# A two-layer hybrid transformer block: values computed for two heads at a time, and part of the conditioning product moved from TensorE to VectorE

## The reference

```python
zx = hx @ w_in[layer]
oa = softmax_attend(q, ka_all, va_all, MLA_SCALE)      # "mla": 4 heads, values 64 wide, latent and context keys
ob = window_gqa_sink(bq, bk, bv, bkc, bvc, sink)       # "swa": 4 query heads on 2 key/value heads, window, sink
oc = diff_attend(dq, dk_all, dv_all, lam)              # "diff": 4 heads, difference of two softmaxes
x = x + mx[2] * rms_norm(concat(oa, ob, oc, od) @ w_out[layer], ...)   # od: pooling group
x = x + mx[5] * rms_norm(hier_moe(modulate(...)), ...)  # 16 experts, top 2 of 4 in the chosen group
```

## Time and profile before

| | |
|---|---|
| Time of three runs | 1197.9, 1199.62, 1202.74 us; median 1199.62 |
| Profiled execution: time, span | 1200.96 us, 1199.1 us |
| Mean granted TensorE clock, share of full | 0.903 |
| TensorE matmul, busy | 950.8 us (79%) |
| VectorE busy | 316.3 us (26%) |
| ScalarE busy | 266.5 us (22%) |
| GpSimd busy | 171.0 us (14%) |
| Moved by DMA | 323.04 MB, mean 269 GB/s |

### The profile page before, as it was taken

How to read it: one execution, slowest core, us unless ns; L and a number is a source line. 1 busy time by engine, 2 the same in 40 slices (tenths; PEclk the granted TensorE clock), 3 DMA queues, 4 the chain that set the end, 5 groups by cost and what they waited for, 6 DMA issues and landing times. The chain is left out here.

```text
span 1199.1 us, 23394 instructions
## 1 busy us (share of the span) xinstructions
PE 950.8 (79%) x8976; PEld 601.0 (50%) x8977; DVE 316.3 (26%) x893; ACT 266.5 (22%) x712; POOL 171.0 (14%) x256
## 2 busy tenths in 40 slices
PE   4899998999997699989974289998996585655561
PEld 2454646766554466656752166657754353422240
DVE  1100064457434211111110420046635110000003
ACT  4121033546332111101100241024632100000001
POOL 0010025000021222211210220013001211100011
PEclk9999997999997799999997599998997788877796
DMA  9982333570175799999999945230129999999983
GB/s 376 333 254 101 140 141 141 211 247 1 34 283 208 274 372 410 410 411 410 411 411 404 357 160 234 107 140 1 38 89 371 374 410 409 410 410 410 409 326 136
DMA packets 97333, 323.04 MB, mean 269 GB/s; under 512 B 11946, under 2 KB 22964, under 8 KB 90996
## 3 DMA queue, kind: packets, MB, share of 16 engines
q1 hardware_dynamic: 70528, 279.19, 59.0%
q0 software_dynamic: 9600, 31.81, 7.8%
q10 hardware_dynamic: 17140, 11.13, 3.0%
HBM read 309.58 MB, written 18.81 MB: 274 GB/s over the span
## 5 line engine op out<-in xcount | busy, mean ns | idle before, releaser
L825 PE MATMUL psum<-weights,lat 128*32 128x256 f32 x2688 | 181.3, 426 | 96.7 <-DMA weights<-in_exp_w_gu_dram 59.5
L825 PEld LDWEIGHTS psum<-weights,lat 128*32 128x32 f32 x2688 | 108.8, 121 | 163.9 <-issue 131.5
L508 PE MATMUL psum<-hT,weights 128*128 128x512 f32 (+1 forms) x336 | 120.7, 518 | 5.6 <-ACT lat L1000 3.2
L1607 DVE STREAM_TRANSPOSE lat<-lat 128x256 f32<-128x256 f32 x66 | 29.4, 446 | 355.1 <-PE psum L825 342.6
L1169 ACT ACTIVATE lat<-psum 128x128 f32<-128x128 f32 x64 | 17.7, 277 | 357.6 <-PE psum L825 355.4
L508 PEld LDWEIGHTS psum<-hT,weights 128*128 128x128 f32 x336 | 64.0, 192 | 59.3 <-issue 49.1
L838 PE MATMUL psum<-weights,lat 128*32 128x256 f32 x1344 | 83.7, 387 | 4.7 <-issue 4.0
L659 PE MATMUL psum<-weights,R 128*128 128x64 f32 x480 | 68.8, 286 | 11.3 <-ACT R L1084 7.1
L1851 POOL DMA_INDIRECT lat<-h_rows,slot_col x68 | 66.5, 978 | 53.9 <-POOL slot_col L1848 53.0
L1380 DVE TENSOR_REDUCE st<-psum 128x1 f32<-128x512 f32 (+1 forms) x96 | 56.7, 599 | 61.9 <-PE psum L628 28.3
L659 PEld LDWEIGHTS psum<-weights,R 128*128 128x128 f32 x480 | 64.2, 205 | 16.1 <-ACT R L1084 10.9
(11 more groups left out here) (260 smaller groups left out, 1161.0 us busy)
## 6 DMA issues: line engine op xcount, KB each, us to landing
weights<-in_exp_w_gu_dram SPq DMA_DIRECT2D x44, 2048.0 KB, 23.9
weights<-in_ada_w_dram SPq DMA_DIRECT2D x24, 2048.0 KB, 8.7
weights<-in_exp_w_down_dram SPq DMA_DIRECT2D x22, 2048.0 KB
hT<-in_exp_w_gu_dram SPq DMA_DIRECT2D x10, 2048.0 KB
R<-in_exp_w_gu_dram SPq DMA_DIRECT2D x10, 2048.0 KB, 25.7
spare_w<-in_exp_w_down_dram SPq DMA_DIRECT2D x10, 2048.0 KB, 24.3
weights<-in_w_in_dram SPq DMA_DIRECT2D x6, 2048.0 KB, 16.5
weights<-in_w_out_dram SPq DMA_DIRECT2D x4, 2048.0 KB, 9.1
```

What stands on the lines that cost most here:

```text
L508: mm = nc.tensor.matmul(t[:, lo:hi], w[:, k, col:col + P], hT[:, k, lo:hi], start=(k == 0), stop=(k == KD - 1))
L825: mm = nc.tensor.matmul(gu_ps[BLK * j:BLK * j + BLK, 0:256], xgT[:, k, :], w[:, k % 4, j, :, :, :], start=(k == 0), stop=(k == KD - 1), sk ...
L1607: nc.vector.transpose(xgT[:, :, :].rearrange("p k s -> p (k s)"), xg[par]).then_inc(x_ready, 1)
```

## The change

**Values by pairs.** For mla and swa units the probabilities are scaled by the reciprocal of their sum before they are turned (VectorE, in `weigh`, in place). The values product then has V as stationary operand, 64 columns wide, and the turned probabilities as the moving one. Two heads are computed together, one in each column half of the array, so that the bank holds the output already turned, head by head in partition halves; ScalarE copies it straight into `mixT` (`pair_out`). `om`, `merge` and VectorE's output scaling stay for diff units alone. There are four `probT` buffers instead of two for mla and swa.

**Layer 1's items 4 to 11.** `ada_fold` on VectorE multiplies each k-block (128 x 2048) with the column of `silu_c` for the latent stream and adds it up in `ada_acc`; `ada_sum` on TensorE then sums over the partitions with a matrix of ones. Group 1 is folded once VectorE has scaled the last rows and the first stream is turned, and is summed after `bq0`; group 2 is folded after the latent is normalised, and is summed after `dv0`. Item 6 waits for the residual, where item 7 did, and four buffers change. As items now stay in `W[0]` until VectorE has used them, ScalarE waits for item 4 before it copies the keys, for item 7 before the diff queries and for item 10 before the latent queries, and GpSimd waits for item 4 before it clears `bqz`.

```diff
-                  (("ada", 1, 6), 1), (("ada", 1, 7), 0), (("in", 1, 3), 3), (("ada", 1, 8), 0), (("ada", 1, 9), 4),
-                  (("ada", 1, 10), 0), (("ada", 1, 11), 5), (("out", 1, 0), 3), (("out", 1, 1), 4)]
+                  (("ada", 1, 6), 0), (("ada", 1, 7), 2), (("in", 1, 3), 3), (("ada", 1, 8), 0), (("ada", 1, 9), 4),
+                  (("ada", 1, 10), 0), (("ada", 1, 11), 4), (("out", 1, 0), 3), (("out", 1, 1), 5)]
...
+            def ada_sum(S, L, r):
+                pe.wait_ge(*at("folded", L, r))
+                reuse(B_ADA, ("ada_sb", L, r))
+                for g in range(4):
+                    mm = nc.tensor.matmul(psum[32 * g:32 * g + 32, B_ADA, :], ones[:, 0:32], ada_acc[:, g * 512:(g + 1) * 512],
+                                          start=True, stop=True, skip_group_check=True)
+                mm.then_inc(*mark(S, ("ada_sum", L, r)))
...
-                        for i in (5, 6):
-                            ada_item(S + "_ada", ("ada", 1, i))
...
-                        ada_item(S + "_ada", ("ada", 1, 7))
...
-                        if used and L:
-                            for i in {1: (8,), 2: (9, 10), 3: (11,)}[c]:
-                                ada_item(S + "_ada", ("ada", 1, i))
-                            if c == 1:
-                                ada_turn(S + "_turn", 1, 1)
+                        if L and name == "bq0":
+                            ada_sum(S + "_ada", 1, 1)
+                        if L and name == "dk1":
+                            ada_turn(S + "_turn", 1, 1)
+                        if L and name == "dv0":
+                            ada_sum(S + "_ada", 1, 2)
...
+                def pair_values(u):
+                    kind, qt, h = U[u]
+                    n, k0 = (4, 0) if qt < 2 else (2, 2)
+                    pe.wait_ge(*at("probT", L, u - 1))
+                    pe.wait_ge(*at("probT", L, u))
+                    if qt == 0 and h == 1:
+                        pe.wait_ge(*at("v", L, kind))
+                    t = take("o", L, u, banks=spare(ring))
+                    for i in range(n):
+                        for b in range(2):
+                            v = {"mla": vas[L][:, k0 + i, (h - 1 + b) * 64:(h + b) * 64],
+                                 "swa": bvs[L][:, k0 + i, (h // 2) * 64:(h // 2) * 64 + 64]}[kind]
+                            mm = nc.tensor.matmul(t[64 * b:64 * b + 64, 0:P], v, turned(L, u - 1 + b)[:, i, :],
+                                                  start=(i == 0), stop=(i == n - 1), skip_group_check=True)
+                    mm.then_inc(*mark(S, ("filled", "o", L, u - 1), ("filled", "o", L, u)))
...
                 if L:
-                    ada_item("pe_comb", ("ada", 1, 4))
                     pe.wait_ge(*at("banks_out", L - 1))
                     turn_combined("pe_comb", L, 0)
...
+                def pair_out(u):
+                    kind, qt, h = U[u]
+                    copy(S, mixT[:, 2 * KINDS.index(kind) + h // 2, qt * P:(qt + 1) * P], ("o", L, u), P)
...
+            def ada_fold(S, L, r):
+                for k in range(KD):
+                    it = ("ada", L, 4 * r + k // 2)
+                    w, c = staged(it)[:, k % 2, :, :].rearrange("p g n -> p (g n)"), silu_c[:, k, 0:1]
+                    used = [("used", item_no[it])] if k % 2 else []
+                    if k % 2 == 0:
+                        v.wait_ge(*at("staged", item_no[it]))
+                    if k == 0:
+                        ts(ada_acc, w, c, None, ALU.mult).then_inc(*mark(S, ("fold", L, r, k)))
+                    else:
+                        v.wait_ge(*at("fold", L, r, k - 1))
+                        stt(ada_acc, w, c, ada_acc, ALU.mult, ALU.add)\
+                            .then_inc(*mark(S, ("fold", L, r, k), *used, *([("folded", L, r)] if k == KD - 1 else [])))
...
                 if L:
+                    ada_rows(S, 1, 1)
+                    ada_fold(S, 1, 2)
+                    ada_columns(S, 1, 1)
                     ada_rows(S, 1, 2)
...
+                    if kind != "diff":
+                        v.wait_ge(*at("rinv", L, u))
+                        p = prob[u % (AHEAD + 1)][:, 0:nk]
+                        ts(p, p, s_[:, 7:8], None, ALU.mult).then_inc(*mark(S, ("prob", L, u)))
...
                 if L:
-                    ada_rows("v_seam", 1, 1)
-                    ada_columns("v_seam", 1, 1)
+                    v.wait_ge(*at("filled", "yT", 1, 0, KD // 2 - 1))
+                    ada_fold("v_seam", 1, 1)
```

More of the change, by code:

```diff
@@ L230, in hybrid_block @@
         prob2 = part(R1, 3 * NTOK, NTOK)
-        probT = [part(R1, (4 + i) * NTOK, NTOK, "p (k q) -> p k q", k=4) for i in range(2)]
         rope_c = [part(R1, 6 * NTOK + i * SEQ, SEQ) for i in range(2)]
         rope_s = [part(R1, 7 * NTOK + i * SEQ, SEQ) for i in range(2)]
+        ada_acc = part(R1, 0, 2 * D)
         h_scaled = [part(R1, i * D, D) for i in range(2)]
@@ L253, in hybrid_block @@
         om = [part(lat, i * 4 * 256, 4 * 256, "p (q c) -> p q c", q=4) for i in range(2)]
+        probT = [part(r, o + i * NTOK, NTOK, "p (k q) -> p k q", k=4) for r, o in ((R1, 4 * NTOK), (lat, 2 * NTOK)) for i in range(2)]
         PADW = 288
@@ L354, in uses, with turned, turned_before @@
             return len(range(place, N_EXP, 3))
+        def turned(L, u):
+            return probT[u % (2 if units(L)[u][0] == "diff" else 4)]
+        def turned_before(L, u):
+            first = 2 * (len(units(L)) // 3)
+            if u < first:
+                return u - 4
+            return first - 4 + (u - first) if u < first + 2 else u - 2
         def units(L):
@@ L656, in values @@
                     for i in range(n):
[L657 to L659 removed]
+                        mm = nc.tensor.matmul(t[:, 0:64], turned(L, u)[:, i, :], dvs[L][:, k0 + i, h * 64:h * 64 + 64], start=(i == 0), stop=(i == n - 1))
                     mm.then_inc(*mark(S, ("filled", "o", L, u)))
[L662 to L670 removed]
                 per = len(U) // 3
```

62 lines of the change are left out of this document (30 added, 32 removed).

## The result

The changed kernel takes 1180.35 us (median of four runs, 1178.45 to 1636.07; the highest one was disturbed, with a granted clock of 0.554, and is not in the ratio, and the median of the other three is 1178.66) against 1198.76 us for the kernel before on the same chip: a ratio of 0.9837, 95% interval [0.9801, 0.9872]. A second submission, `after_again`, gave 1177.94 us and 0.9851 [0.9808, 0.9895]. The forecast of 1176 us with 1168 to 1190 around it holds. The profiled execution took 1178.45 us, its span is 1176.6, 22.5 less than before; 24.2 were forecast.

What follows compares the result with a forecast made beforehand. TensorE bounds the seam and attention, with VectorE loaded at attention's starts; weight traffic bounds the experts. Savings of 13.0 (seam), 7.0 (layer 0) and 4.2 (layer 1), 24.2 us, off 1200.96, less 1.3 to the median, give 1176 us, range 1168 to 1190.

Steps and rivals of the forecast that it cites:

- Part 1, the seam: Between the layers: taking layer 1's items 4 to 11 off TensorE saves 13.0 us.
- Items 5 and 6 lie where TensorE would otherwise wait for that chain: nothing for them: In the seam: removing these two items saves nothing, since TensorE would wait there for the chain behind the first turning.
- The folds: VectorE in the seam: 2.4 us a step, ends near 717.5 and 762, hidden, some 1.5 us to spare at the second.
- Rivals B and E: Seam: second fold or its loads late, 1182 us, chance 0.1; first fold late or blocking ScalarE, 1188 us, 0.03.
- Part 2, the price of a pair: Values product in attention: 16 instructions at 0.058 us plus 0.1, so 1.03 us a pair, 0.68 saved.
- Rival A: Values product: column halves no faster, 0.110 us an instruction as in bq, a full pair 1.86 us; 1189 us, chance 0.15.
- Part 3, the step that failed: Attention: VectorE's scaling of probabilities, about 0.45 us a unit, is hidden in steady windowed units but not at stage starts.
- Rival C: Attention: VectorE's scaling binds at the contended 0.72 us, and both starts lose 2 us more each; 1181 us, chance 0.1.
- The starts: Start of each attention stage: longer VectorE queue from the new scaling costs 1.2 us in layer 1, 0.7 in layer 0.
- Layer 0: Its attention saves 7.0 us: full units 4.1, context-only 1.1, half-clock pairs 0.7, merges' transposes 1.75, less 0.7 at the start.
- Rival D: Attention: emptier TensorE stays longer at half clock; 1206 us if 30 us of full-rate work run so; chance 0.04.
- One listed sign of being wrong: Granted clock of 0.5 past the attention stages' starts would show the forecast wrong.

Runs made afterwards that it cites:

- `a_pairs_only`: Changed kernel with the folds undone: items 4 to 11 on TensorE again, in the old order of loads; values by pairs stay. 1188.95 us.
- `b_fold_only`: Changed kernel with the pairs undone: `om` and `merge` back, probabilities unscaled; the folds on VectorE stay. 1181.31 us.
- `e_halves_apart`: Changed kernel with all of one head's values instructions before the other's, instead of alternating; median 7.5 us above the changed kernel's second submission.
- `c_pairs_later`: Changed kernel with TensorE multiplying a pair one step later and ScalarE taking its output one step later; 1166.91 us.
- `d_copy_first`: Changed kernel with ScalarE copying the turned probabilities before the next exponential, for non-differential units; 1166.51 us.
- `h_split_on_act`: `d_copy_first` with the quarter scalings of the late differential queries moved from VectorE to ScalarE; 1154.94 us.
- `k_all`: `h_split_on_act` plus seven additional matmuls, result unused, ahead of the second turning in the seam; 1156.21 us.
- `m_before_split`: Kernel before the change, with only the late differential queries' quarter scalings moved from VectorE to ScalarE; 1186.31 us against 1199.57.

## Why the prediction held, and where it did not

**The total** is right, partly by luck. The forecast took 13.0 us from the seam, 7.0 from layer 0 and 4.2 from layer 1. The spans show 10.4, 13.8 and 0.1; the rest, 2.2 lost behind layer 1's attention and 0.4 gained elsewhere, makes 22.5. Two terms fell short, and the clock of layer 0's attention made up for them.

**Part 1, the seam: right in mechanism, 2.6 us too large.** Item 4 ahead of the first turning was worth 5.9 us (from layer 0's third pair of loads to the turning, 265.3 before and 259.4 after) against 5.4. The items in the busy stretch less the sums (1.0 us each against 0.9) were worth 6.9 between ckv's end and layer 1's first scores, where 9.1 - 1.8 + 0.3 = 7.6 stood. Most of what was missing is between the two: the second turning and ckv ran wholly or in part at the half clock, 1.7 us more for ckv and 0.7 in the chain ahead of it. "Items 5 and 6 lie where TensorE would otherwise wait for that chain: nothing for them" counted their time and gave the clock after them no term; with them there, ckv had taken 3.69 us in the kernel before, but 6.66 in `a_pairs_only`. So these 2.4 us are the clock's, and whether the items' going caused them is not shown. Between `a_pairs_only` and `after_again` the seam is 12.6 us shorter, between the kernel before and `b_fold_only` 9.5; the forecast's 13.0 is at the upper end.

**The folds**: step (2.4), both ends, the hiding and the sums without a wait came as written. VectorE did wait for weights, 3.77 us in the first fold and 1.21 to 1.40 three times in the second, inside the margin. Rivals B and E are refuted by the missing brackets at L495 and by the seam's gain of 10.4 us.

**Part 2, the price of a pair: right** (1.03 us against 1.03), and `e_halves_apart` shows that having both halves in flight is what brings it. The exact match is luck: 16 x 0.054 is 0.86 us and going in and out 0.17, where 0.93 and 0.1 stood. Rival A is refuted. Its bound, bq's 0.110 us, is indeed bq's moving columns.

**Part 3, the step that failed**: "Probabilities are turned three units after their scores, so the longer path is hidden." The distance was counted in units, where it had to be counted in the orders of two engines. Before, every step had a values product of 0.84 us, and the copy of unit i - 4 was needed one step after it was turned. Now even steps have no product, odd steps need the copies of two units, and the younger of them stands in ScalarE behind an exponential that itself waits for maxima. This cost 0.72 us a pair in steady windowed units, all of the 0.68 that a pair saved, and more before the pairs at the stages' starts. `c_pairs_later` and `d_copy_first` give it back, 11 us. A period is then 4.05 us where 3.94 was forecast. Some 0.09 of that stand in the turning ahead of a pair, which in `c_pairs_later` takes 0.53 us (802.75 to 803.28) against 0.44 for the other one (805.38 to 805.82): going into the split array costs something ahead of the pair as well, and no term had it. Rival C named the right place for the wrong cause: a doubled scaling costs steady units nothing. Its price of 1181 us is near the measured 1180.35 by chance.

**The starts**: the forecast put the loss to the new scaling, 1.2 us in layer 1 and 0.7 in layer 0. In layer 1 TensorE's idle time ahead of the pairs among the windowed scores rose from 3.4 to 6.6 us, so by 3.2; in `d_copy_first` it is 4.4, so 1.0 more than before. The term was nearly right for what VectorE's queue adds, and the other 2.2 us are the copy's place again. The stalls themselves were there before the change (3.92 us in layer 0 and 2.21 in layer 1). Layer 1's whole account: 6.2 us of work gone, and 3.2 us of idle time more at the start, 1.7 before pairs among the windowed scores and 1.2 behind them.

**Layer 0**: against `b_fold_only` the pairs gained 7.3 us (1.5 of it the clock at most), where 7.0 was forecast, with waits of 0.6 to 1.0 us before some pairs inside it. `a_pairs_only`, with the changed kernel's code in this stage, took 147.7, so 4.3 less than `b_fold_only`. An estimate with the clock out, half of the us at the half level taken off each: 148.0 and 149.0 without the pairs, 143.1 and 142.5 with them, a gain of 5 to 6.5 us. Rival D, the clock, went the other way in this stage. One listed sign of being wrong came once and not again: the granted clock of 0.50 past the starts, at `w_out` from 867 to 874 us. The chance that the clock should help had no place in the forecast, though the earlier trace rows and the clock of 0.50 from 824 to 830 us show stalls that the kernel before paid for twice.

## What to carry to other kernels

When two steps' work is joined into one, write down for both engines what stands in their queues between producing and using each operand: a distance of three units was none, since the copy stood behind another unit's exponential, and a change of order gave back 11 us for no work. After a saving on the engine that seems to bind, compare its busy time and the stage's length in the same window; where the first falls (81.9 to 75.7) and the second does not (85.5 to 85.4), the gain is in new waits. And look at short stalls at a stage's start together with the clock behind them: moving sixteen small instructions from VectorE to ScalarE was worth 11.6 us with the change, and up to 13.3 without it.

## What the runs showed of the hardware

Unchanged code can run several us faster or slower by the granted clock alone: layer 0's attention took 158.5 us at 0.94 and 152.0 at 0.98. The kernel before has runs from 1189 to 1203 us, a wider spread than what the pairs alone gained (10 us). Its 51 later runs fall into two groups: 17 took 1189.1 to 1195.1 us, with a mean granted clock of 0.905 to 0.912, and 34 took 1197.6 to 1203.5, with 0.896 to 0.906. Its profile (1200.96) is one of the second kind, so every difference to it above is against the longer of the two. With the stalls at the start removed, the clock was 1.00 in both attention stages of `h_split_on_act` and `k_all`, and their runs lay within 1153.8 to 1158.0; `m_before_split`, with 0.99 and 1.00, has runs from 1183.0 to 1189.2.

With two column halves in flight together an instruction of 128 moving columns takes 0.054 us, and with one half alone 0.11, with the same operands. Going into the split array and out again cost some 0.17 us a pair, and 0.09 more in the instructions ahead of it.

A scaling of 128x2048 on VectorE takes 1.28 us, or 1.59 in the first fold, and a multiply-add of that width 2.4. Four scalings of 128x256 take 1.84 us on ScalarE in `h_split_on_act`, and 1.65 or 2.91 on VectorE.
